# A pair's expert results added to their tokens by one-hot products, in place of rows scattered and read back

## The chip, the cores and the metric

One core of a Trainium2 chip. The metric is device time in microseconds (us) of one execution of the whole program; lower is better. Five engines work beside each other: TensorE (PE in the profile; its weight loads are PEld), VectorE (DVE), ScalarE (ACT), GpSimd (POOL) and SyncE (SP, which here issues the weight loads). They meet only through semaphores.

## What is computed

A backbone of two layers over 256 latent and 256 context tokens of width 1024. Layer 0 mixes tokens by windowed attention, layer 1 by a bidirectional linear recurrence; behind each stands a mixture of experts, and at the end a root-mean-square norm. What matters here is the mixture of layer 1, which sees the 256 latent tokens only. Its reference, cut to what matters:

```python
scores = sigmoid(t @ router_w)                       # 64 experts
idx    = top 8 of 64, within the best 4 of 8 groups
w      = scores[idx] / sum(scores[idx]) * 2.5
y      = (silu(t @ w_gate[e]) * (t @ w_up[e])) @ w_down[e] * w_b      # t: tokens of a block, one expert e
routed = zeros((T + 1, D)).at[tok_buf].add(y)        # each token: the sum of its 8 results
x      = x + g2 * (routed + shared)
return rms_norm(x, final_g)
```

256 tokens by 8 experts make 2048 results of 1024 numbers. All is float32; an expert has three matrices of 1 MB each.

## The kernel before

The program runs phases one behind the other, each a block in which every engine has its own list of instructions; a block ends when all engines have ended. `route_phase` chooses the experts and sorts (token, expert) entries into blocks of 64 slots; it also adds the shared expert into `g.x` and starts the first weight loads. `expert_pair_phase` (lines 1535 to 1796) is the stage of the change. `combine_phase` (1798 to 1880) sums the results, applies the gate, adds to the stream and does the final norm. `combine_phase` also serves layer 0, where nothing changes.

In `expert_pair_phase` a step handles a pair of blocks, 2 x 64 slots, one half of the 128 partitions each; there are 33 pairs. Slots without an entry have gain 0 and an index out of range. The first pair is peeled, the others run two to a turn of a loop. For pair i:

- GpSimd gathers 128 token rows into `xg` by an indirect DMA (`gather`, line 1617; rows out of range are skipped, and the tile was cleared once at line 1628). After the results are out of PSUM it scatters them to `y_rows` in device memory (`scatter`, line 1625), a row for each token and choice.
- TensorE (`step`, lines 1678 to 1704) projects gate and up (line 1674, weights loaded two pairs ahead into one of two buffers), transposes the tokens of pair i+1 (1666), looks up the slots of pair i+2 by a one-hot product (1654), transposes the hidden rows (1691), and multiplies by the down weights (1702), of which there is one buffer. Float32 matmuls show as two instructions each in the trace; projections and down product run as two halves of 64 columns side by side.
- ScalarE: SiLU (1725), half of the transposed tokens (1719), the transposed hidden rows (1728), half of the result (1732). VectorE: gain and product (1775), the other half of the tokens (1768), the indices (1760, 1763, 1781), the next one-hot (1748), the other half of the result (1783).
- SyncE issues the weight loads (926, 929, 932) in the order in which buffers come free: gate and up two pairs ahead, when the projections are done; down of pair i+1 when the down product of pair i is done.

All loads of the weights stand in one queue, in the order of issue. The order of work on each engine is written out by hand, as the lists show; nothing plans it at run time.

`combine_phase` reads `y_rows` back, four rows of a token at a time in four loads of 2 MB (line 1832); TensorE sums half of a tile's rows by products with the identity (1852), VectorE the other half (1867, 1869, 1872); then gate (1874), addition to the stream (1876) and the norm (ScalarE 328 and 330, VectorE 335 and 337), and the output is stored (1840).

Of the kernel before, what the change touches and what calls it, by code (L numbers as in the profile page):

```python
# [29 lines left out]
P = 128  # L30
# [1503 lines left out]

def expert_pair_phase(g, layer, tiles, routes, weights):

# [4 lines left out]
    S = slots_of(tiles)  # L1541
    last_token, last_row = tiles * P - 1, tiles * P * TOPK - 1
    half = (slice(0, S), slice(S, 2 * S))
    with ExitStack() as st:
        sb = lambda n, s, d=F32: st.enter_context(nc.sbuf_tensor(f"{tag}_{n}", s, d))
        sem = lambda n: g.sem(f"{tag}_{n}")
        wgu, wd = weights.wgu, weights.wd
        xg, ysb = g.h[:, 0, :], g.h[:, 2, :]
        xT = sb("xT", [P, KD, P])
        onehot = sb("onehot", [P, tiles, P], BF16)  # L1550
        meta = sb("meta", [P, NBMAX // 2, 3])
        gidx = sb("gidx", [P, 1], U32)
        sidx = sb("sidx", [P, 1], U32)
        act_g = sb("act_g", [P, FE])
        hid = sb("hid", [P, FE])
        hidT = sb("hidT", [P, KF, P])
        gathered, scattered, zeroed, issue = sem("gathered"), sem("scattered"), sem("zeroed"), sem("issue")
        onehot_s, meta_done, meta_v, idx_s = sem("onehot_s"), sem("meta_done"), sem("meta_v"), sem("idx_s")
        xT_turned, xT_a, xT_v = sem("xT_turned"), sem("xT_a"), sem("xT_v")
        gate_done, up_done, silued, hid_s = sem("gate_done"), sem("up_done"), sem("silued"), sem("hid_s")  # L1560
        hid_turned, hidT_s, y_done = sem("hid_turned"), sem("hidT_s"), sem("y_done")
        y_a, y_v, sidx_s = sem("y_a"), sem("y_v"), sem("sidx_s")
        GU, YB, XB, HB, MB = 0, 1, 3, 5, 6

# [10 lines left out]
        def peeled(i):  # L1575
            return isinstance(i, int) and i == 0

        with nc.Block() as block:
# [31 lines left out]
            @block.gpsimd  # L1610
            def _(pool):
                def gather(i):
                    pool.wait_ge(idx_s, i + 1)
                    if not peeled(i):
                        pool.wait_ge(xT_turned, i)
                    pool.sem_inc(issue, 1)
                    pool.indirect_dma_start(xg, None, g.h2_rows[0:tiles * P, :], bass.IndirectOffsetOnAxis(ap=gidx[:, 0:1], axis=0),
                                            bounds_check=last_token, oob_is_err=False).then_inc(gathered, 16)

                def scatter(i):  # L1620
                    pool.wait_ge(y_a, i + 1)
                    pool.wait_ge(y_v, i + 1)
                    pool.wait_ge(sidx_s, i + 1)
                    pool.sem_inc(issue, 1)
                    pool.indirect_dma_start(g.y_rows[0:tiles * P * TOPK, :], bass.IndirectOffsetOnAxis(ap=sidx[:, 0:1], axis=0), ysb, None,
                                            bounds_check=last_row, oob_is_err=False).then_inc(scattered, 16)

                pool.memset(xg, 0.0).then_inc(zeroed, 1)
                pool.wait_ge(zeroed, 1)
                turns = rounds(pool)  # L1630
                gather(0)
                gather(1)
                gather(2)
                scatter(0)
                with pool.Fori(0, turns) as m:
                    gather(2 * m + 3)
                    scatter(2 * m + 1)
                    gather(2 * m + 4)
                    scatter(2 * m + 2)
                pool.wait_ge(scattered, 32 * turns + 16)  # L1640
                pool.sem_inc(issue, 1)
                pool.wait_ge(gathered, 32 * turns + 48)
                pool.sem_inc(issue, 1)

            @block.tensor
            def _(pe):
# [21 lines left out]

                def project(q, r, a, loaded, done):
                    pe.wait_ge(loaded[q], 32 * r + 32)  # L1670
                    pe.sem_inc(issue, 1)
                    for k in range(KD):
                        for s in range(2):
                            last = pe.matmul(g.ps[half[s], GU, a * FE:(a + 1) * FE], xT[:, k, half[s]], wgu[:, q, s, a, k, :],  # L1674
                                             start=(k == 0), stop=(k == KD - 1))
                    last.then_inc(done, 1)

                def step(i, q, r):
# [5 lines left out]
                    project(q, r, 0, weights.gate_in, gate_done)  # L1684
                    project(q, r, 1, weights.up_in, up_done)
                    turn_tokens(i + 1)
                    slots(i + 2)
                    pe.wait_ge(hid_s, i + 1)
                    pe.sem_inc(issue, 1)
                    for j in range(KF):  # L1690
                        last = pe.transpose(g.ps[:, HB, j * P:(j + 1) * P], hid[:, j::KF], g.ident)
                    last.then_inc(hid_turned, 1)
                    pe.wait_ge(hidT_s, i + 1)
                    pe.wait_ge(weights.down_in, 32 * i + 32)
                    if not peeled(i):
                        pe.wait_ge(y_a, i)
                        pe.wait_ge(y_v, i)
                    pe.sem_inc(issue, 1)
# [12 lines left out]
                with pe.Fori(0, turns) as m:  # L1711
                    step(2 * m + 1, 1, m)
                    step(2 * m + 2, 0, m + 1)

            @block.scalar
            def _(act):
# [4 lines left out]
                def step(i):  # L1721
# [7 lines left out]
                    act.wait_ge(y_done, i + 1)  # L1729
                    if not peeled(i):  # L1730
                        act.wait_ge(scattered, 16 * i)
                    act.activation(ysb[:, 0:512], g.ps[:, YB, :], ACT.Copy).then_inc(y_a, 1)  # L1732

# [8 lines left out]
            def _(dve):  # L1742
# [23 lines left out]
                def tokens(i):  # L1766
                    dve.wait_ge(xT_turned, i + 1)
                    dve.tensor_copy(xT[:, 4:8, :], g.ps[:, XB + 1, :].rearrange("p (k c) -> p k c", c=P)).then_inc(xT_v, 1)  # L1768

                def step(i):  # L1770
                    dve.wait_ge(silued, i + 1)
                    dve.wait_ge(meta_v, 2 * i + 2)
                    if not peeled(i):
                        dve.wait_ge(hid_turned, i)
                    dve.scalar_tensor_tensor(hid[:], act_g[:], meta[:, bass.ds(i, 1), GAIN], g.ps[:, GU, FE:2 * FE], ALU.mult, ALU.mult).then_inc(hid_s, 1)  # L1775
                    tokens(i + 1)
                    indices(i + 2)
                    pick(i + 3)
                    if not peeled(i):
                        dve.wait_ge(scattered, 16 * i)  # L1780
                    dve.tensor_scalar(sidx[:], meta[:, bass.ds(i, 1), DEST], FAR, None, ALU.add).then_inc(sidx_s, 1)
                    dve.wait_ge(y_done, i + 1)
                    dve.tensor_copy(ysb[:, 512:D], g.ps[:, YB + 1, :]).then_inc(y_v, 1)  # L1783

# [3 lines left out]
                indices(1)  # L1788
                pick(2)
                tokens(0)  # L1790
                turns = rounds(dve)
                step(0)
                with dve.Fori(0, turns) as m:
                    step(2 * m + 1)
                    step(2 * m + 2)


def combine_phase(g, layer, tiles):
# [7 lines left out]
    with ExitStack() as st:  # L1806
# [15 lines left out]
        with nc.Block() as block:  # L1822
# [40 lines left out]
            def _(dve):  # L1863
                for t in range(tiles):
# [12 lines left out]
                    if t:  # L1877
                        dve.wait_ge(mod_in, 32 if layer == 0 else 16)
                        norm.dve(dve, t - 1)
                norm.dve(dve, tiles - 1)  # L1880


# [401 lines left out]
def backbone(nc, ins, table, out):  # L2284
    with ExitStack() as stack:
# [39 lines left out]
        with ExitStack() as layer:  # L2325
# [13 lines left out]
            with ExitStack() as moe:  # L2339
# [3 lines left out]
                turned.close()  # L2343
                expert_pair_phase(g, 1, LAT_TILES, routes, weights)
            combine_phase(g, 1, LAT_TILES)

# [69 lines left out]
```

## Time and profile before

| | us |
|---|---|
| median of 3 runs | 2253.72 (2251.86 to 2254.84) |
| the profiled execution | 2252.88 |
| its span in the trace | 2251.1 |
| second expert stage | about 1644 to 2205 |
| combination, norm and output | 2213 to 2251 |

| busy over the span | us | share |
|---|---|---|
| TensorE, matmul | 1853.2 | 82% |
| VectorE | 1116.1 | 50% |
| ScalarE | 797.5 | 35% |
| GpSimd | 315.8 | 14% |

The span runs from the first to the last instruction; the time of an execution has a little around it (1.8 us here). A busy share over the whole span mixes stages with different limits, so each stage is to be read by itself: busy time of each engine in the stretch, share of the 16 DMA engines, and which wait of the pacing engine ends last. The granted clock of TensorE is given as a share of full speed (0.5 is 1.2 GHz, 1.0 is 2.4 GHz).

### The profile page before, as it was taken

To read this page: it belongs to the slowest core of one execution; us is meant where nothing else is said; L and a number is where in the kernel's file an instruction comes from. 1 tells how busy PE (TensorE), PEld (TensorE's weight loads), DVE (VectorE), ACT (ScalarE), POOL (GpSimd) and SP (SyncE) were. 2 spreads that over 40 slices of the span, in tenths; PEclk is the share of its full clock that TensorE was granted. 3 is DMA by queue.
4 is the path that set the end of the run, shared out by engine and by line. 5 is a ranking of instruction groups with operands and counts; after the bars stand their busy time and mean duration, and the time that the engine had idled before them with its cause. 6 is when DMAs were issued, how large, how long until landed. Compare 5 with 4: busy or idle time off the path is not lost. (4 is left out here: it accounts for less than half of the span.)

```text
span 2251.1 us, 32259 instructions
## 1 busy us (share of the span) xinstructions
PE 1853.2 (82%) x9555; PEld 1210.6 (54%) x9556; DVE 1116.1 (50%) x1942; ACT 797.5 (35%) x1283; POOL 315.8 (14%) x333
## 2 busy tenths in 40 slices
PE   2899997979999999999966977638778778788884
PEld 0778853556767676766633961113445445455451
DVE  1425632477877777777836656891321111111113
ACT  1214511045656565666612547850101111111111
POOL 0220010011111111112211012220011111111110
PEclk9999988889999999999987988758879899999997
DMA  6860053258999999999956334304659999999984
GB/s 247 273 216 12 1 186 138 118 184 343 365 361 351 352 356 372 365 360 358 359 213 244 94 79 172 113 10 131 256 209 405 399 409 400 414 406 401 408 333 197
DMA packets 128296, 597.10 MB, mean 265 GB/s; under 512 B 32633, under 2 KB 51129, under 8 KB 67441
## 3 DMA queue, kind: packets, MB, share of 16 engines
q1 hardware_dynamic: 92512, 509.97, 58.7%
q0 software_dynamic: 35584, 84.32, 10.2%
q10 hardware_dynamic: 144, 2.10, 0.2%
q8 instruction: 32, 0.52, 0.1%
q14 instruction: 24, 0.19, 0.0%
HBM read 596.18 MB, written 56.20 MB: 290 GB/s over the span
## 5 line engine op out<-in xcount | busy, mean ns | idle before, releaser
L1484 DVE TENSOR_TENSOR m_w_lo<-mods,m_w_hi 128x1024 fp32r<-128x1024 f32 x264 | 311.6, 1222 | 27.4 <-ACT m_w_hi L1403 24.7
L1403 ACT ACTIVATE m_w_hi<-mods 128x1024 fp32r<-128x1024 f32 x264 | 263.7, 1049 | 13.9 <-PEq L995 12.0
L1355 PE MATMUL ps<-m_w_hi,m_x_hi 128*128 128x512 f32 x528 | 245.1, 464 | 5.6 <-DVE m_x_lo L1476 5.6
L1339 PE MATMUL ps<-m_wd,m_hidT 128*128 128x512 f32 x528 | 248.1, 592 | 0.9 <-DVE h L1492 0.9
L1702 PE MATMUL ps<-m_wd,m_hidT 128*64 128x512 f32 x528 | 163.5, 775 | 92.8 <-DMA m_wd<-in_moe_w_down 91.4
L1674 PE MATMUL ps<-m_wgu,m_xT 128*64 128x256 f32 x2112 | 236.7, 382 | 1.2 <-DVE m_xT L1768 1.2
L1674 PEld LDWEIGHTS ps<-m_wgu,m_xT 128*64 128x64 f32 x2112 | 175.0, 138 | 71.3 <-issue 21.2
L1355 PE MATMUL ps<-m_w_lo,m_x_hi 128*128 128x512 f32 x528 | 208.1, 394 | 0.0
L1355 PE MATMUL ps<-m_w_hi,m_x_lo 128*128 128x512 f32 x528 | 207.0, 392 | 0.0
L1702 PEld LDWEIGHTS ps<-m_wd,m_hidT 128*64 128x64 f32 x528 | 52.3, 176 | 180.2 <-issue 180.2
L1339 PEld LDWEIGHTS ps<-m_wd,m_hidT 128*128 128x128 f32 x528 | 95.5, 191 | 70.8 <-issue 63.6
L1775 DVE SCALAR_TENSOR_TENSOR m_hid<-m_act_g,m_meta,ps 128x256 f32<-128x256 f32 x33 | 15.8, 480 | 233.3 <-ACT m_act_g L1725 233.3
L1271 POOL DMA_INDIRECT h<-h_rows,m_gidx x69 | 72.8, 1055 | 342.8 <-DVE m_gidx L1468 337.8
L1355 PEld LDWEIGHTS ps<-m_w_hi,m_x_hi 128*128 128x128 f32 x528 | 100.0, 189 | 35.4 <-issue 21.3
L1355 PEld LDWEIGHTS ps<-m_w_hi,m_x_lo 128*128 128x128 f32 x528 | 100.3, 190 | 29.7 <-issue 15.3
L1355 PEld LDWEIGHTS ps<-m_w_lo,m_x_hi 128*128 128x128 f32 x528 | 99.5, 188 | 22.7
L328 ACT ACTIVATE squares<-x_stream 128x1024 bf16<-128x1024 f32 x16 | 16.9, 1053 | 264.4 <-DVE x_stream L867 140.8
L1783 DVE COPY h<-ps 128x512 f32<-128x512 f32 x33 | 22.8, 691 | 172.5 <-PE ps L1702 172.5
L1732 ACT ACTIVATE h<-ps 128x512 f32<-128x512 f32 x33 | 19.7, 597 | 246.2 <-PE ps L1702 246.2
L1280 POOL DMA_INDIRECT y_rows<-h,m_sidx x66 | 66.9, 1014 | 216.9 <-DVE h L1492 211.0
L1476 DVE TENSOR_TENSOR m_x_lo<-ps,m_x_hi 128x512 fp32r<-128x512 f32 x134 | 85.8, 681 | 5.9 <-ACT m_x_hi L1393 5.9
L1725 ACT ACTIVATE m_act_g<-ps 128x256 f32<-128x256 f32 x33 | 12.6, 383 | 210.9 <-PE ps L1674 210.9
(322 smaller groups left out, 3262.2 us busy)
## 6 DMA issues: line engine op xcount, KB each, us to landing
m_wd<-in_moe_w_down SPq DMA_DIRECT2D x132, 1024.0 KB, 11.1
mods<-in_moe_w_gate SPq DMA_DIRECT2D x66, 1024.0 KB, 7.0
mods<-in_moe_w_up SPq DMA_DIRECT2D x66, 1024.0 KB, 10.5
m_wgu<-in_moe_w_gate SPq DMA_DIRECT2D x66, 1024.0 KB, 11.2
m_wgu<-in_moe_w_up SPq DMA_DIRECT2D x66, 1024.0 KB, 13.5
c_rows<-y_rows SPq DMA_DIRECT2D x12, 2048.0 KB, 14.4
mods<-in_ada_w POOLq DMA_DIRECT2D x11, 1024.0 KB, 6.2
mods<-in_ada_w SPq DMA_DIRECT2D x11, 1024.0 KB, 4.9
```

Of the source, the lines that this page charges most:

```text
L328: act.activation(g.junk[:], g.x[:, t, :], ACT.Square, accum_out=g.sumsq[:, t:t + 1]).then_inc(self.squared, 1)
L1271: pool.indirect_dma_start(xg[q], None, g.h2_rows[0:tiles * P, :], bass.IndirectOffsetOnAxis(ap=gidx[q][:, 0:1], axis=0), bounds_check=last ...
L1280: pool.indirect_dma_start(g.y_rows[0:tiles * P * TOPK, :], bass.IndirectOffsetOnAxis(ap=sidx[q][:, 0:1], axis=0), ysb[q], None, bounds_che ...
L1339: last = pe.matmul(g.ps[0:S, YB + n, :], hidT[:, q, j, :], wd[:, q, j, n * 512:(n + 1) * 512], start=(j == 0), stop=(j == KF - 1))
L1355: last = pe.matmul(g.ps[0:S, GU, :].rearrange("p (a f) -> p a f", a=2), x[:, q, k, :], w[:, q, :, k, :], start=(k == 0 and n == 0), stop=( ...
L1403: act.activation(w_hi[:, q, :, k, :], wgu[:, q, :, k, :], ACT.Copy).then_inc(hi_s, 1)
L1476: dve.tensor_tensor(x_lo[:, q, ks, :], g.ps[:, XB + n, 0:4 * S].rearrange("p (k c) -> p k c", c=S), x_hi[:, q, ks, :].bitcast(F32), ALU.su ...
L1484: dve.tensor_tensor(w_lo[:, q, :, k, :], wgu[:, q, :, k, :], w_hi[:, q, :, k, :].bitcast(F32), ALU.subtract).then_inc(lo_s, 1)
L1674: last = pe.matmul(g.ps[half[s], GU, a * FE:(a + 1) * FE], xT[:, k, half[s]], wgu[:, q, s, a, k, :], start=(k == 0), stop=(k == KD - 1))
L1702: last = pe.matmul(g.ps[half[s], YB + n, :], hidT[:, j, half[s]], wd[:, s, j, n * 512:(n + 1) * 512], start=(j == 0), stop=(j == KF - 1))
L1732: act.activation(ysb[:, 0:512], g.ps[:, YB, :], ACT.Copy).then_inc(y_a, 1)
L1783: dve.tensor_copy(ysb[:, 512:D], g.ps[:, YB + 1, :]).then_inc(y_v, 1)
```

## The change

The results of a pair stay on the chip. ScalarE copies them from PSUM rounded to the short float format (float32r, `y_hi`), VectorE takes the remainder (`y_lo`). VectorE also makes a matrix `place` of 128 slots by 256 tokens, 1 where the slot's token is the column's. TensorE multiplies `place` with `y_hi` and `y_lo` into one PSUM bank (`put`), in four jobs (two tiles of tokens by two halves of the width), and VectorE adds each into a sum of 128x2x1024 in SBUF (`add`). The puts of pair i-1 stand among the work of pair i: the first behind the gate projection, the second in the middle of the up projection, the third behind the transposes of the tokens, the fourth behind those of the hidden rows. The sum and two tables are set up at the start of the stage. GpSimd issues no scatter, and clears the token tile ahead of each gather. `finish_phase` takes the place of `combine_phase` in layer 1. The diff, cut to its core:

```diff
--- before.py
+++ after.py
...
-def expert_pair_phase(g, layer, tiles, routes, weights):
+def expert_pair_phase(g, layer, tiles, routes, weights, total):
-        xg, ysb = g.h[:, 0, :], g.h[:, 2, :]
+        xg = g.h[:, 0, :]
-        sidx = sb("sidx", [P, 1], U32)
+        y_hi, y_lo = sb("y_hi", [P, D], F32R), sb("y_lo", [P, D], F32R)
+        place = sb("place", [P, tiles * P], F32R)
+        tokens_far = sb("tokens_far", [P, tiles, P])
+        jobs = [(t, n) for t in range(tiles) for n in range(2)]
+        J = len(jobs)
-        GU, YB, XB, HB, MB = 0, 1, 3, 5, 6
+        GU, YB, XB, HB, MB, TB = 0, 1, 3, 5, 6, 7
...
             def _(pool):
                 def gather(i):
-                    pool.wait_ge(idx_s, i + 1)
                     if not peeled(i):
                         pool.wait_ge(xT_turned, i)
                     pool.sem_inc(issue, 1)
+                    pool.memset(xg, 0.0).then_inc(zeroed, 1)
+                    pool.wait_ge(zeroed, i + 1)
+                    pool.wait_ge(idx_s, i + 1)
+                    pool.sem_inc(issue, 1)
                     pool.indirect_dma_start(xg, None, g.h2_rows[0:tiles * P, :], bass.IndirectOffsetOnAxis(ap=gidx[:, 0:1], axis=0),
                                             bounds_check=last_token, oob_is_err=False).then_inc(gathered, 16)
-                def scatter(i):
-                    pool.wait_ge(y_a, i + 1)
-                    pool.wait_ge(y_v, i + 1)
-                    pool.wait_ge(sidx_s, i + 1)
-                    pool.sem_inc(issue, 1)
-                    pool.indirect_dma_start(g.y_rows[0:tiles * P * TOPK, :], bass.IndirectOffsetOnAxis(ap=sidx[:, 0:1], axis=0), ysb, None,
-                                            bounds_check=last_row, oob_is_err=False).then_inc(scattered, 16)
-
-                pool.memset(xg, 0.0).then_inc(zeroed, 1)
-                pool.wait_ge(zeroed, 1)
                 turns = rounds(pool)
                 gather(0)
                 gather(1)
                 gather(2)
-                scatter(0)
                 with pool.Fori(0, turns) as m:
                     gather(2 * m + 3)
-                    scatter(2 * m + 1)
                     gather(2 * m + 4)
-                    scatter(2 * m + 2)
-                pool.wait_ge(scattered, 32 * turns + 16)
                 pool.wait_ge(gathered, 32 * turns + 48)
                 pool.sem_inc(issue, 1)
...
                         last = pe.transpose(g.ps[:, XB + k // 4, (k % 4) * P:(k % 4 + 1) * P], xg[:, k::KD], g.ident)
                     last.then_inc(xT_turned, 1)
-                def project(q, r, a, loaded, done):
+                def put(i, n, bank):
+                    t, half_of_d = jobs[n]
+                    if n == 0:
+                        pe.wait_ge(placed, i + 1)
+                        pe.wait_ge(y_low, i + 1)
+                    pe.wait_ge(added, J * i + n + 1)
+                    pe.sem_inc(issue, 1)
+                    for m, y in enumerate((y_hi, y_lo)):
+                        last = pe.matmul(g.ps[:, bank, :], place[:, t * P:(t + 1) * P], y[:, half_of_d * 512:(half_of_d + 1) * 512],
+                                         start=(m == 0), stop=(m == 1))
+                    last.then_inc(put_done, 1)
+                def project(q, r, a, loaded, done, inside=None):
                     pe.wait_ge(loaded[q], 32 * r + 32)
                     pe.sem_inc(issue, 1)
                     for k in range(KD):
+                        if k == KD // 2 and inside:
+                            inside()
                         for s in range(2):
                             last = pe.matmul(g.ps[half[s], GU, a * FE:(a + 1) * FE], xT[:, k, half[s]], wgu[:, q, s, a, k, :],
                                              start=(k == 0), stop=(k == KD - 1))
...
                     if not peeled(i):
                         pe.wait_ge(hid_s, i)
                     project(q, r, 0, weights.gate_in, gate_done)
-                    project(q, r, 1, weights.up_in, up_done)
+                    if peeled(i):
+                        project(q, r, 1, weights.up_in, up_done)
+                    else:
+                        put(i - 1, 0, TB)
+                        project(q, r, 1, weights.up_in, up_done, inside=lambda: put(i - 1, 1, TB))
                     turn_tokens(i + 1)
+                    if not peeled(i):
+                        put(i - 1, 2, TB)
                     slots(i + 2)
                     pe.wait_ge(hid_s, i + 1)
                     pe.sem_inc(issue, 1)
                     for j in range(KF):
                         last = pe.transpose(g.ps[:, HB, j * P:(j + 1) * P], hid[:, j::KF], g.ident)
                     last.then_inc(hid_turned, 1)
+                    if not peeled(i):
+                        put(i - 1, 3, TB)
                     pe.wait_ge(hidT_s, i + 1)
                     pe.wait_ge(weights.down_in, 32 * i + 32)
-                    if not peeled(i):
-                        pe.wait_ge(y_a, i)
-                        pe.wait_ge(y_v, i)
                     pe.sem_inc(issue, 1)
                     for j in range(KF):
                         for n in range(2):
...
                 with pe.Fori(0, turns) as m:
                     step(2 * m + 1, 1, m)
                     step(2 * m + 2, 0, m + 1)
+                for n in range(J):
+                    put(2 * turns, n, TB)
             @block.scalar
             def _(act):
...
                     act.wait_ge(hid_turned, i + 1)
                     act.activation(hidT[:], g.ps[:, HB, 0:KF * P].rearrange("p (j c) -> p j c", c=P), ACT.Copy).then_inc(hidT_s, 1)
                     act.wait_ge(y_done, i + 1)
-                    if not peeled(i):
-                        act.wait_ge(scattered, 16 * i)
-                    act.activation(ysb[:, 0:512], g.ps[:, YB, :], ACT.Copy).then_inc(y_a, 1)
+                    act.activation(y_hi[:], g.ps[:, YB:YB + 2, :].rearrange("p a b -> p (a b)"), ACT.Copy).then_inc(y_high, 1)
                 tokens(0)
                 turns = rounds(act)
...
                     dve.wait_ge(xT_turned, i + 1)
                     dve.tensor_copy(xT[:, 4:8, :], g.ps[:, XB + 1, :].rearrange("p (k c) -> p k c", c=P)).then_inc(xT_v, 1)
+                def add(i, n):
+                    t, half_of_d = jobs[n]
+                    part = total[:, t, half_of_d * 512:(half_of_d + 1) * 512]
+                    dve.wait_ge(put_done, J * i + n + 1)
+                    dve.tensor_tensor(part, part, g.ps[:, TB, :], ALU.add).then_inc(added, 1)
                 def step(i):
+                    if not peeled(i):
+                        add(i - 1, 0)
+                        add(i - 1, 1)
                     dve.wait_ge(silued, i + 1)
                     dve.wait_ge(meta_v, 2 * i + 2)
                     if not peeled(i):
                         dve.wait_ge(hid_turned, i)
                     dve.scalar_tensor_tensor(hid[:], act_g[:], meta[:, bass.ds(i, 1), GAIN], g.ps[:, GU, FE:2 * FE], ALU.mult, ALU.mult).then_inc(hid_s, 1)
                     tokens(i + 1)
+                    if not peeled(i):
+                        add(i - 1, 2)
                     indices(i + 2)
                     pick(i + 3)
                     if not peeled(i):
-                        dve.wait_ge(scattered, 16 * i)
-                    dve.tensor_scalar(sidx[:], meta[:, bass.ds(i, 1), DEST], FAR, None, ALU.add).then_inc(sidx_s, 1)
-                    dve.wait_ge(y_done, i + 1)
-                    dve.tensor_copy(ysb[:, 512:D], g.ps[:, YB + 1, :]).then_inc(y_v, 1)
+                        add(i - 1, 3)
+                    dve.tensor_scalar(place[:], tokens_far[:].rearrange("p t c -> p (t c)"), meta[:, bass.ds(i, 1), 0], None, ALU.is_equal).then_inc(placed, 1)
+                    dve.wait_ge(y_high, i + 1)
+                    dve.tensor_tensor(y_lo[:], g.ps[:, YB:YB + 2, :].rearrange("p a b -> p (a b)"), y_hi[:].bitcast(F32), ALU.subtract).then_inc(y_low, 1)
                 pick(0)
                 indices(0)
                 pick(1)
                 indices(1)
                 pick(2)
+                for t in range(tiles):
+                    dve.tensor_scalar(tokens_far[:, t, :], g.field("iota"), t * P - FAR, None, ALU.add).then_inc(far_s, 1)
+                dve.wait_ge(far_s, tiles)
+                dve.memset(total, 0.0).then_inc(added, 1)
                 tokens(0)
                 turns = rounds(dve)
                 step(0)
                 with dve.Fori(0, turns) as m:
                     step(2 * m + 1)
                     step(2 * m + 2)
+                for n in range(J):
+                    add(2 * turns, n)
...
+def finish_phase(g, tiles, total):
+        gain = st.enter_context(nc.sbuf_tensor("fin_gain", [P, D], F32))
+        norm = NormRows(g, "nf", None, lambda t: gain[:])
+        with nc.Block() as block:
+            @block.sync
+            def _(sp):
+                sp.dma_start(gain[:], g.ins["final_g"].partition_broadcast(P)).then_inc(gain_in, 16)
+                for t in range(tiles):
+                    sp.wait_ge(norm.ready, t + 1)
+                    sp.dma_start(g.out[0, t * P:(t + 1) * P, :], g.h[:, t, :]).then_inc(stored, 16)
+                sp.wait_ge(stored, 16 * tiles)
+            @block.scalar
+            def _(act):
+                for t in range(tiles):
+                    act.wait_ge(added, t + 1)
+                    norm.act(act, t)
+            @block.vector
+            def _(dve):
+                for t in range(tiles):
+                    dve.tensor_tensor(total[:, t, :], total[:, t, :], g.mod(t, GATE2), ALU.mult).then_inc(scaled, 1)
+                    dve.wait_ge(scaled, t + 1)
+                    dve.tensor_tensor(g.x[:, t, :], g.x[:, t, :], total[:, t, :], ALU.add).then_inc(added, 1)
+                dve.wait_ge(gain_in, 16)
+                for t in range(tiles):
+                    norm.dve(dve, t)
...
                 routes, weights = Routes(sb, 1, LAT_TILES), PairWeights(g, sb, 1)
                 route_phase(g, 1, LAT_TILES, routes, weights)
-                expert_pair_phase(g, 1, LAT_TILES, routes, weights)
-            combine_phase(g, 1, LAT_TILES)
+                total = g.h[:, 1::2, :]
+                expert_pair_phase(g, 1, LAT_TILES, routes, weights, total)
+            finish_phase(g, LAT_TILES, total)
```

## Rows read from the trace of the kernel before

**Rows 1.** Busy time by stretch: length, then busy us (count) of PE, PEld, DVE, ACT, POOL, clock, DMA share, GB/s

```profile
1665.00:1670.00 5.00, 4.56 (x27) 2.33 (x29) 1.87 (x8) 0.89 (x3) 0.99 (x1) 1.00 1.02 428
...
1800.00:2000.00 200.00, 161.31 (x1128) 100.20 (x1124) 34.57 (x111) 23.53 (x48) 24.30 (x25) 0.91 1.00 407
```

**Rows 2.** The waits of TensorE, 1660 to 2210 us: us in total, times, longest

```profile
PE ps L1702 <- DMA m_wd<-in_moe_w_down: 91.4, 31, 5.1
```

**Rows 3.** The DMA queues and issues, 1800 to 2150 us

```profile
q1 hardware_dynamic: 18089, 131.72, 92.1%
q0 software_dynamic: 6048, 10.75, 8.0%
...
h<-h_rows,m_gidx POOLq DMA_INDIRECT x22, 8.3
```

**Rows 4.** The timeline (start, us, instruction, [idle before]), TensorE's down products

```profile
1680.29 6.47 PE L1702 MATMUL ps<-m_wd,m_hidT 128*64 128x512 f32 x16 [2.31 <-DMA m_wd<-in_moe_w_down]
...
2184.34 5.33 PE L1702 MATMUL ps<-m_wd,m_hidT 128*64 128x512 f32 x16 [3.69 <-DMA m_wd<-in_moe_w_down]
...
2199.22 3.65 PE L1702 MATMUL ps<-m_wd,m_hidT 128*64 128x512 f32 x16 [0.78 <-ACT m_hidT L1728]
```

**Rows 5.** The timeline, the last pair, 2189 to 2199 us

```profile
2189.49 7.09 PE L1674 MATMUL ps<-m_wgu,m_xT 128*64 128x256 f32 x64
...
2196.51 0.97 PEld L1666 LDWEIGHTS ps<-table,h 128*128 128x128 f32 x8 [0.38 <-issue]
...
2197.74 0.68 DVE L1768 COPY m_xT<-ps 128x512 f32<-128x512 f32 x1
...
2197.96 0.47 PE L1691 MATMUL ps<-table,m_hid 128*128 128x128 f32 x2 [0.20 <-DVE m_hid L1775]
...
2198.48 0.38 ACT L1728 ACTIVATE m_hidT<-ps 128x256 f32<-128x256 f32 x1 [0.17 <-PE ps L1691]
```

**Rows 6.** The timeline, float32r matmuls of layer 0, around 800 us

```profile
800.14 0.39 PE L1355 MATMUL ps<-m_w_hi,m_x_hi 128*128 128x512 f32 x1
...
800.37 0.39 PE L1355 MATMUL ps<-m_w_hi,m_x_lo 128*128 128x512 f32 x1
```

**Rows 7.** Groups by line (count | busy, mean ns | idle before), whole span

```profile
L1403 ACT ACTIVATE m_w_hi<-mods 128x1024 fp32r<-128x1024 f32 x264 | 263.7, 1049 | 13.9 <-PEq L995 12.0
...
L1476 DVE TENSOR_TENSOR m_x_lo<-ps,m_x_hi 128x512 fp32r<-128x512 f32 x134 | 85.8, 681 | 5.9 <-ACT m_x_hi L1393 5.9
...
L759 DVE MEMSET lo_w<- 32x2048 f32 x4 | 7.1, 1765 | 1.9 <-issue 1.1 <-PEq L2122 0.8
```

**Rows 8.** The timeline, start of the stage, 1640 to 1661 us

```profile
1640.45 1.23 DVE L1093 TENSOR_TENSOR x_stream<-x_stream,h 128x1024 f32<-128x1024 f32 x1
...
1641.96 0.96 POOL L1628 MEMSET h<- 128x1024 f32 x1 [117.77 <-POOLq L995]
...
1652.94 0.69 DVE L1768 COPY m_xT<-ps 128x512 f32<-128x512 f32 x1
...
1653.73 9.56 PE L1674 MATMUL ps<-m_wgu,m_xT 128*64 128x256 f32 x64 [1.22 <-DVE m_xT L1768]
...
1660.10 0.89 SPq L926 DMA_DIRECT2D m_wgu<-in_moe_w_gate  x2
```

**Rows 9.** The timeline, end of the stage and combination

```profile
2202.99 0.60 ACT L1732 ACTIVATE h<-ps 128x512 f32<-128x512 f32 x1 [4.13 <-PE ps L1702]
...
2204.49 0.99 POOL L1625 DMA_INDIRECT y_rows<-h,m_sidx  x1 [3.73 <-DVE h L1783]
...
2213.17 0.81 SPq L1832 DMA_DIRECT2D c_rows<-y_rows  x2
...
2235.32 1.28 ACT L330 ACT_TABLE_LOAD   x1
...
2242.51 1.22 DVE L1874 TENSOR_TENSOR c_total<-c_total,mods 128x1024 f32<-128x1024 f32 x1
...
2245.03 1.06 ACT L328 ACTIVATE squares<-x_stream 128x1024 bf16<-128x1024 f32 x1 [8.12 <-DVE x_stream L1876]
```

More of the change, by code:

```diff
@@ L1541, in expert_pair_phase @@
     S = slots_of(tiles)
-    last_token, last_row = tiles * P - 1, tiles * P * TOPK - 1
+    last_token = tiles * P - 1
     half = (slice(0, S), slice(S, 2 * S))
@@ L1556, in expert_pair_phase @@
         hidT = sb("hidT", [P, KF, P])
-        gathered, scattered, zeroed, issue = sem("gathered"), sem("scattered"), sem("zeroed"), sem("issue")
+        gathered, zeroed, issue = sem("gathered"), sem("zeroed"), sem("issue")
         onehot_s, meta_done, meta_v, idx_s = sem("onehot_s"), sem("meta_done"), sem("meta_v"), sem("idx_s")
@@ L1561, in expert_pair_phase @@
         hid_turned, hidT_s, y_done = sem("hid_turned"), sem("hidT_s"), sem("y_done")
-        y_a, y_v, sidx_s = sem("y_a"), sem("y_v"), sem("sidx_s")
-        GU, YB, XB, HB, MB = 0, 1, 3, 5, 6
+        y_high, y_low, placed = sem("y_high"), sem("y_low"), sem("placed")
+        put_done, added, far_s = sem("put_done"), sem("added"), sem("far_s")
+        GU, YB, XB, HB, MB, TB = 0, 1, 3, 5, 6, 7
         def rounds_after_first(eng):
@@ L1633, in _ @@
                 gather(2)
-                scatter(0)
                 with pool.Fori(0, turns) as m:
                     gather(2 * m + 3)
-                    scatter(2 * m + 1)
                     gather(2 * m + 4)
-                    scatter(2 * m + 2)
-                pool.wait_ge(scattered, 32 * turns + 16)
-                pool.sem_inc(issue, 1)
                 pool.wait_ge(gathered, 32 * turns + 48)
@@ L1880, in _ @@
                 norm.dve(dve, tiles - 1)
+def finish_phase(g, tiles, total):
+    nc = g.nc
+    with ExitStack() as st:
+        gain = st.enter_context(nc.sbuf_tensor("fin_gain", [P, D], F32))
+        gain_in, stored = g.sem("fin_gain_in"), g.sem("fin_stored")
+        scaled, added = g.sem("fin_scaled"), g.sem("fin_added")
+        norm = NormRows(g, "nf", None, lambda t: gain[:])
[21 more added lines that the diff above has]
+                    norm.dve(dve, t)
 BA, BX, LAM, CW, CB = 0, 2, 4, 6, 10
```

## The prediction

> **What bounds the kernel now.** I read the table of busy time by stretch first. In the second expert stage (about 1644 to 2205 us) the row of 1800 to 2000 us has the DMA engines at a share of 1.00 and 407 GB/s, TensorE busy 161 of 200 us, VectorE 35, ScalarE 24, GpSimd 24 [rows 1]. So the stage is paced by transfers. The waits say which: TensorE waited 31 times, 91.4 us in all, for the down weights before line 1702 [rows 2]. The list of DMA queues splits the 350 us from 1800 to 2150: the hardware queue (weights) took 92.1% of the 16 engines' time, the software queue (22 gathers, 21 scatters) 8.0%, together 100% [rows 3]. The starts of the down product give the period: from 1680.29 to 2184.34 us are 30 pairs, 504.05 / 30 = 16.80 us each [rows 4].
>
> TensorE's own chain is shorter. The last pair did not wait for weights: 2184.34 to 2199.22 is 14.88 us, of which the down product at 2184.34 took 5.33 where the one at 2199.22 took 3.65 (part of it ran at the lower of the two clocks, after an idle stretch); at full clock the chain is 14.88 - 1.68 = 13.2 us [rows 4]. Nearly 3.6 us per pair are to spare. After the last pair comes the combination: TensorE ends at 2199.22 + 3.65 = 2202.87, the span at 2251.1, so 48.2 us of tail [rows 4, 9].
>
> **Part 1, the scatters go.** 8.0% of 350 us is 28.0 us for 43 software transfers, 0.65 us each of all 16 engines' time [rows 3]. Nothing else limits the period as long as TensorE's chain is below it, and the next down load is issued about 11 us before it lands, so the queue never runs dry. 31 scatters (pairs 0 to 30) are sent before the last down load that TensorE waits for. Gain 31 x 0.65 = 20.2 us, period 16.80 - 0.65 = 16.15. Bounds: nothing, if weights move no faster without scatters; at most, weights at the 428 GB/s of 1665 to 1670 us, when mostly weights moved [rows 1]: 131.72 MB / 21 = 6.27 MB per pair, 14.65 us instead of 15.35, another 0.7 us per pair or 22 us. I take 20.2, since the 5 us stretch is short and the gathers stay.
>
> **Part 2, what is added to each pair.** TensorE gets eight single-pass matmuls of 128x512 (four puts of two). Line 1355 runs the same kind and type: starts 0.23 us apart at full clock [rows 6], so a put holds TensorE 0.45 us. Put 0 stands behind the gate projection. It needs ScalarE's rounded copy of 128x1024 (1.05 us by line 1403) and VectorE's remainder (2 x 0.68 by line 1476, taken as 1.25) [rows 7], done 2.5 us after the down product; the gate projection lasts half of 7.09 = 3.5 us [rows 5], so it hides them, with 1 us over. Put 1 comes 1.8 us later in the up projection, and its accumulator bank is free again after 0.69 us of adding; no wait. With 0.1 us each for the wait instruction these two add 1.1 us. Put 2 follows the transposes; nobody waits but TensorE. Put 3 waits for the add of put 2, which VectorE does only behind its copy of the transposed tokens: in the last pair's times that copy ends at 2197.74 + 0.68 = 2198.42, the add at 2199.15, put 3 at 2199.75, where the down product began at 2199.22 [rows 4, 5]; so puts 2 and 3 together cost 0.6 us, the rest falls into the wait for ScalarE's transposed hidden rows (2198.48 + 0.38). Chain: 13.2 + 1.1 + 0.6 = 14.9 us, under 16.15. In the 31 pairs bound by transfers this costs nothing; without that cover it is 1.7 us per pair. It shows once, in the last pair: +1.7. It also shortens idle stretches, so fewer down products should drop to the lower clock; that too is hidden.
> VectorE gets four adds of 0.69, one product-mask of 256 columns and the remainder instead of a copy: 2.8 + 0.4 + 0.6, some 3.7 us on 3.5 busy per 16.8; no bound. The add in front of the index arithmetic makes the gather about 0.7 us later; a gather lands 8.3 us after issue [rows 3] of a period of 16.15, and goes out some 4 us after the transposes, so about 4 us are left. GpSimd's memset of the token tile, 0.96 us [rows 8], runs after the transposes while VectorE still computes the indices (about 1.2 us): hidden, or at worst 1 us later for the same gather. Down products no longer wait for evacuation; put 0's wait has covered that.
>
> **Part 3, the start.** VectorE now fills two token tables and clears a 128x2048 sum before its first copy of transposed tokens (1652.94), on which the first projection (1653.73) hangs, and on that the third pair's gate load at 1660.10, with which the saturated stretch begins [rows 8]. Clearing: 1.8 us by line 759's 2048 columns [rows 7]; tables about 0.25 each. +2.3 us, bounds 1.2 (clearing at twice the rate) and 5 (if the later start leaves TensorE longer at the lower clock, at which most of its first projection of 9.56 us already ran).
>
> **Part 4, the tail.** After the last down product: copy and remainder 0.1 + 1.05 + 0.1 + 1.25 = 2.5 us, then four rounds through one bank: two matmuls 0.6, add 0.69, two hand-overs 0.15, 1.45 us each; 1.9 at the lower clock. Four are 5.8 to 7.6, taken as 6.5: 9.0 us. The change of phase is 0.4: at the phase before, GpSimd's memset began 0.3 us after VectorE's last add [rows 8]; bounds 0 and 4. Before, the same point (line 1832's first issue at 2213.17) was 10.3 us after the down product, scatter included [rows 9]. The new phase: multiply, add, multiply, add at 1.22 each [rows 9] are 5.0 us. ScalarE squares tile 0 from 2.5 (1.06, 0.2 for the sum, 1.28 for the table load, 0.3), so it ends tile 1 at 7.1 instead of the 1.5 us behind the second add that it takes now. Before, from the second multiply (2242.51) to the end were 8.6 us [rows 9]; now 2.5 + 8.6 + 0.6 = 11.7. The 512 KB of gains are moved by then. Tail 9.0 + 0.4 + 11.7 = 21.1 against 48.2: gain 27.1, bounds 22 and 29.
>
> **Sum.** The profiled execution took 2252.88 us (span 2251.1): 2252.88 - 20.2 + 1.7 + 2.3 - 27.1 = 2209.6. The median of the runs is 0.84 above that execution, so 2210.
>
> **A rule that speaks against it.** Going from the half-width projections to the full-width transposes, TensorE shows no gap: the projections run from 2189.49 for 7.09 us, the weight load of the transposes begins at 2196.51, after 0.38 us without a weight load [rows 5]. The Trainium skill's page "TensorEngine Tiling (Array Packing)", Key Properties, says that changing the tiling mode drains the engine. Puts 0 and 1 lie inside half-width work, four more changes per pair; by that rule something like the 0.38 us would be lost at each, by the row nothing. That makes it a rival, below.
>
> **The rivals.**
> - TensorE's chain becomes the bound. Four changes of array width at 0.38 us are 1.5 us: chain 16.4, over 16.15; 0.25 x 30 + 1.5 + 2210 = 2219. With slow down products added (1.7 us in many pairs now [rows 4]) up to 17.0: 2236. Against: no gap between the kinds now, and less idle time to lose the clock in.
> - The weights gain more than the scatters' own time, as 428 GB/s hints: half of that bound, 0.35 x 31 = 11 us, gives 2199. Against: a share of 1.00 at 407 GB/s in all long stretches.
> - The change doesn't shorten the stage, since the weight queue alone sets the period and scatters fit in between: 2210 + 20 = 2230. Against: both queues' shares add up to 100%.
> - Slower than before: the one accumulator bank makes TensorE and VectorE take turns. If VectorE, in order behind its waits for the activation and the transposes, is late at each add, every put costs a full round of 1.45 us and puts 1 to 3 hold up projections and down product: 13.2 + 4 x 1.45 = 19.0 us, 2.85 more than 16.15, 31 times: 2210 + 88 = 2298. It decides from a chain of 16.15 + 43 / 31 = 17.6 us on. Against: 1.8 us of projection stand between puts 0 and 1, 2 us between 1 and 2.
>
> **Chances.** Forecast 0.64 (own range 2203 to 2217), TensorE's chain 0.18, faster weights 0.10, unshortened stage 0.04, slower 0.04. Under 0.2% (4.5 us) this kernel can't be told from unchanged; only tails of the rivals end there, 0.01. Faster 0.95, slower 0.04. Range 2195 to 2229.
>
> **What would show it.** Right: starts of the down product 16.1 us apart, DMA share still 1.00, TensorE still waiting about 1 us for down weights in most pairs, software queue's share about half, first gate load of the third pair near 1662.5, 21 us from the last down product to the end. Wrong: no more waits for down weights (TensorE is the bound); a period still of 16.8 with those waits (scatters cost nothing); a first projection much later than 1656; rounds of the last four adds over 2 us.

## The result and the profile after

The changed kernel takes 2198.26 us (median of 4 runs, 2193.9 to 2200.84) against 2254.28 (4 runs); the ratio is 0.975, 95% interval 0.973 to 0.977. Timed again later it took 2195.66 (5 runs), ratio 0.976 (0.975 to 0.978). Forecast were 2210 us and a range of 2195 to 2229: right in sign and range, but the gain is 56 us, not 44. The profiled execution took 2200.84 us, span 2199.0; it is the slowest of the four, so the profiles differ by less (52.1 us) than the medians.

The waits of TensorE in the stage (us in total, times, longest), against [rows 2]:

```profile
PE ps L1670 <- DVE h L1786: 20.4, 32, 0.7
PE ps L1714 <- DMA m_wd<-in_moe_w_down: 5.6, 10, 0.7
```

91.4 us of waiting for down weights have become 5.6. Line 1670 is the put, and what it waits for is the add of the put before it. The row of 1800 to 2000 us and the DMA queues of 1800 to 2120 us, against [rows 1, 3]:

```profile
1800.00:2000.00 200.00, 188.38 (x1303) 109.72 (x1299) 79.22 (x164) 30.27 (x52) 24.32 (x25) 1.00 1.01 413
```

```profile
q1 hardware_dynamic: 17503, 127.45, 96.7%
q0 software_dynamic: 3003, 5.28, 4.4%
```

The engines of the DMA are as full as before, the weights have 96.7% of them instead of 92.1%, and TensorE is granted full speed, here and in every stretch from 1670 to 2175 us. Some starts of the down product, against [rows 4]:

```profile
1685.46 3.65 PE L1714 MATMUL ps<-m_wd,m_hidT 128*64 128x512 f32 x16
...
1716.44 3.65 PE L1714 MATMUL ps<-m_wd,m_hidT 128*64 128x512 f32 x16
...
1731.52 0.40 PE L1670 MATMUL ps<-m_y_lo,m_place 128*128 128x512 f32 x1
1732.03 3.65 PE L1714 MATMUL ps<-m_wd,m_hidT 128*64 128x512 f32 x16
1748.22 3.65 PE L1714 MATMUL ps<-m_wd,m_hidT 128*64 128x512 f32 x16 [0.62 <-DMA m_wd<-in_moe_w_down]
...
2172.60 0.40 PE L1670 MATMUL ps<-m_y_lo,m_place 128*128 128x512 f32 x1
2172.93 3.65 PE L1714 MATMUL ps<-m_wd,m_hidT 128*64 128x512 f32 x16
```

From 1732.03 the next start is 16.2 us away, with a wait for weights that the list holds. From 1716.44 it is 15.6 us away, and that period has a wait too, too short for the list: the down product starts 0.51 us behind the last matmul of the put, where it starts 0.33 us behind it in the last period (2172.60 to 2172.93). That last period, 15.4 us, is TensorE's own chain (15.4 and 15.5 by turns in the loop). The mean is (2157.52 - 1685.46) / 30 = 15.74 us: TensorE is 0.3 us per pair faster than the transfers, and waits a little for them in most pairs.

Since the code up to the stage is the same in all kernels here, but its end moved between 1637.8 and 1643.7 us from profile to profile, I count from that end (VectorE's last addition of the shared expert). In us, from one profile of each kernel:

| kernel | first projection | second down product | 30 periods (mean) | last period | last down product to end | all |
|---|---|---|---|---|---|---|
| before | 12.1 | 38.6 | 504.1 (16.80) | 14.9 | 51.9 | 609.4 |
| changed | 15.2 | 42.5 | 472.1 (15.74) | 15.4 | 26.1 | 556.1 |
| changed, again | 15.4 | 42.7 | 472.3 (15.74) | 15.4 | 25.3 | 555.7 |
| before, no scatter | 12.2 | 37.7 | 473.2 (15.77) | 14.9 | 47.8 | 573.6 |
| before, empty scatter | 12.0 | 37.6 | 477.7 (15.92) | 13.2 | 52.0 | 580.5 |
| changed + scatter | 15.1 | 42.6 | 507.2 (16.91) | 15.4 | 25.9 | 591.0 |
| changed + second gather | 17.1 | 43.6 | 500.8 (16.69) | 15.4 | 25.7 | 585.4 |
| three banks | 15.2 | 42.0 | 471.5 (15.72) | 15.0 | 21.5 | 549.9 |
| clearing on GpSimd | 12.2 | 39.3 | 471.5 (15.72) | 15.4 | 26.1 | 552.2 |
| clearing on GpSimd, again | 11.9 | 39.2 | 471.4 (15.71) | 15.4 | 26.1 | 552.0 |
| both | 11.8 | 38.6 | 471.3 (15.71) | 14.9 | 21.5 | 546.4 |
| both, again | 12.1 | 38.7 | 471.7 (15.72) | 14.9 | 21.9 | 547.2 |

The 52.1 us between the two spans are: +1.2 ahead of the stage (not the change's), +3.9 to the second down product, -32.0 over 30 periods, +0.5, -25.8 at the end.

One period of the changed kernel on TensorE and VectorE, against [rows 5]:

```profile
2149.06 0.50 PE L1670 MATMUL ps<-m_y_hi,m_place 128*128 128x512 f32 x1
2149.39 0.40 PE L1670 MATMUL ps<-m_y_lo,m_place 128*128 128x512 f32 x1
2149.72 1.95 PE L1681 MATMUL ps<-m_wgu,m_xT 128*64 128x256 f32 x16
...
2154.14 1.16 PE L1659 MATMUL ps<-table,h 128*128 128x128 f32 x8
...
2155.47 0.68 DVE L1780 COPY m_xT<-ps 128x512 f32<-128x512 f32 x1
...
2156.07 0.68 DVE L1786 TENSOR_TENSOR h<-h,ps 128x512 f32<-128x512 f32 x1
...
2156.89 0.47 PE L1670 MATMUL ps<-m_y_hi,m_place 128*128 128x512 f32 x1 [0.68 <-DVE h L1786]
...
2157.52 3.65 PE L1714 MATMUL ps<-m_wd,m_hidT 128*64 128x512 f32 x16
```

Put 0 holds TensorE from 2149.06 to 2149.72; its matmuls start 0.33 us apart, where line 1355's did 0.23 [rows 6]. Put 3 waits, as worked out, for the add behind the token copy. The start of the stage, against [rows 8]:

```profile
1654.08 0.94 DVE L1814 TENSOR_SCALAR m_tokens_far<-table 128x128 f32<-128x128 f32 x2
1655.52 1.76 DVE L1816 MEMSET h<- 128x2048 f32 x1 [0.49 <-DVE m_tokens_far L1814]
1657.31 0.69 DVE L1780 COPY m_xT<-ps 128x512 f32<-128x512 f32 x1
1658.11 9.69 PE L1681 MATMUL ps<-m_wgu,m_xT 128*64 128x256 f32 x64 [4.34 <-DVE m_xT L1780]
```

And its end, against [rows 9]: the second and third of the four rounds, then the new phase.

```profile
2181.33 0.76 PE L1670 MATMUL ps<-m_y_hi,m_place 128*128 128x512 f32 x1 [0.87 <-DVE h L1786]
2181.89 0.63 PE L1670 MATMUL ps<-m_y_lo,m_place 128*128 128x512 f32 x1
2182.55 0.69 DVE L1786 TENSOR_TENSOR h<-h,ps 128x512 f32<-128x512 f32 x1 [1.38 <-PE ps L1670]
2183.39 0.77 PE L1670 MATMUL ps<-m_y_hi,m_place 128*128 128x512 f32 x1 [0.87 <-DVE h L1786]
...
2187.70 1.23 DVE L1942 TENSOR_TENSOR h<-h,mods 128x1024 f32<-128x1024 f32 x1 [0.32 <-PEq L1583]
```

### The profile page after: what moved, and what is told of

The parts are those of the page before. It is cut to its first block and busy times, and to the rows that moved or that the text cites. A ratio compares the mean times of both kernels' runs of the same rounds, so it can differ in the third digit from the quotient of the medians.

```text
span 2199.0 us, 33098 instructions
## 1 busy us (share of the span) xinstructions
PE 1885.2 (86%) x9787; PEld 1211.7 (55%) x9788; DVE 1221.3 (56%) x2071; ACT 811.3 (37%) x1283; POOL 321.7 (15%) x334
## 5 line engine op out<-in xcount | busy, mean ns | idle before, releaser
L1403 ACT ACTIVATE m_w_hi<-mods 128x1024 fp32r<-128x1024 f32 x264 | 263.9, 1049 | 20.8 <-PEq L995 11.9
L1681 PE MATMUL ps<-m_wgu,m_xT 128*64 128x256 f32 x2112 | 251.1, 385 | 4.3 <-DVE m_xT L1780 4.3
L1681 PEld LDWEIGHTS ps<-m_wgu,m_xT 128*64 128x64 f32 x2112 | 160.9, 138 | 96.2 <-issue 46.7
L1786 DVE TENSOR_TENSOR h<-h,ps 128x512 f32<-128x512 f32 x132 | 90.5, 685 | 124.8 <-PE ps L1670 123.8
L1271 POOL DMA_INDIRECT h<-h_rows,m_gidx x69 | 79.4, 1151 | 349.9 <-DVE m_gidx L1468 345.4
L1714 PE MATMUL ps<-m_wd,m_hidT 128*64 128x512 f32 x528 | 120.6, 597 | 7.1 <-DMA m_wd<-in_moe_w_down 5.6
L1621 POOL MEMSET h<- 128x1024 f32 x35 | 33.3, 952 | 525.4 <-PE ps L1659 407.0
L1744 ACT ACTIVATE m_y_hi<-ps 128x1024 fp32r<-128x1024 f32 x33 | 33.8, 1023 | 157.6 <-PE ps L1714 157.6
L1670 PE MATMUL ps<-m_y_hi,m_place 128*128 128x512 f32 x132 | 65.3, 495 | 25.7 <-DVE h L1786 23.0
```

Source lines behind the costliest of these rows:

```text
L1271: pool.indirect_dma_start(xg[q], None, g.h2_rows[0:tiles * P, :], bass.IndirectOffsetOnAxis(ap=gidx[q][:, 0:1], axis=0), bounds_check=last ...
L1403: act.activation(w_hi[:, q, :, k, :], wgu[:, q, :, k, :], ACT.Copy).then_inc(hi_s, 1)
L1670: last = pe.matmul(g.ps[:, bank, :], place[:, t * P:(t + 1) * P], y[:, half_of_d * 512:(half_of_d + 1) * 512], start=(m == 0), stop=(m == 1))
L1714: last = pe.matmul(g.ps[half[s], YB + n, :], hidT[:, j, half[s]], wd[:, s, j, n * 512:(n + 1) * 512], start=(j == 0), stop=(j == KF - 1))
L1744: act.activation(y_hi[:], g.ps[:, YB:YB + 2, :].rearrange("p a b -> p (a b)"), ACT.Copy).then_inc(y_high, 1)
L1786: dve.tensor_tensor(part, part, g.ps[:, TB, :], ALU.add).then_inc(added, 1)
```

## The experiments

The question was why a scatter is worth 1.06 us per pair when its own packets take 0.65. Theory A: beside its own time it costs the weights theirs. Theory B: the rest comes from TensorE's steadier rhythm at full clock, which sends the down loads off more evenly. All four kernels were timed on one chip, before at 2252.33.

**1. Before, without scatters.**

```diff
-                    pool.indirect_dma_start(g.y_rows[...], ..., ysb, None, ...).then_inc(scattered, 16)
+                    pool.sem_inc(scattered, 16)
```

> The kernel before without the scatters (GpSimd only counts the semaphore up; the combination then sums rows that this layer did not write). TensorE's work, its idle stretches and its falls to the lower clock stay. Theory A, a scatter costs the weight transfers more than its own packets' time: the period of the down products falls from 16.80 us to about 15.75, as in the changed kernel, 31 x 1.05 = 33 us less in the stage, and some 5 us less at the change of phase: about 2216 us. Theory B, the scatter costs only its 0.65 us and the other 0.4 us came from TensorE's steadier rhythm at full clock: period 16.15, about 2228 us.

2215.89 us, ratio 0.984 (0.982 to 0.986); period 15.77. Its queues from 1800 to 2120 us and TensorE's waits from 1680 to 2170:

```profile
q1 hardware_dynamic: 17548, 127.79, 96.7%
q0 software_dynamic: 2880, 5.09, 4.2%
```

```profile
PE ps L1700 <- DMA m_wd<-in_moe_w_down: 68.9, 30, 3.8
```

TensorE idles 2.3 us per pair and still falls to the lower clock (0.94 granted from 1800 to 2120 us, 0.91 before), and yet the period is the changed kernel's. Theory B falls: the stage's gain is the scatter's alone.

**2. Before, with empty scatters.**

```diff
-  dve.tensor_scalar(sidx[:], meta[:, bass.ds(i, 1), DEST], FAR, None, ALU.add)
+  dve.tensor_scalar(sidx[:], meta[:, bass.ds(i, 1), DEST], 2 * FAR, None, ALU.add)
```

> The kernel before with every row of the scatters out of range: descriptors are made and sent, no result is written (the combination sums rows that this layer did not write). If the written data are what costs (A): period near that without scatters, 15.8 to 16.0 us, about 2220 us. If the descriptors of a software transfer cost as much as its data: about 16.3 us, 2235 us. Theory B says no lower than 16.15.

2221.87 us, ratio 0.986 (0.985 to 0.988); period 15.92. Twice the packets of experiment 1 and the same megabytes:

```profile
q1 hardware_dynamic: 17404, 126.74, 95.9%
q0 software_dynamic: 5760, 5.10, 4.8%
```

Descriptors without data cost 0.15 us per pair over none at all, the data 16.80 - 15.92 = 0.88. Every instruction and every wait of the kernel before is still there, so it is not the order of the work or the waits on the scatter that cost. Its last period, with both down products at full clock, is 13.2 us: the chain that the prediction worked out for TensorE.

**3. The changed kernel, with the scatter beside it.**

```diff
+  def scatter(i):
+      pool.wait_ge(y_high, i + 1)
+      pool.wait_ge(sidx_s, i + 1)
+      pool.indirect_dma_start(g.y_rows[...], ..., y_hi[:].bitcast(F32), None, ...).then_inc(scattered, 16)
```

> The changed kernel, with each pair's rounded results also scattered to device memory as before (nobody reads them). Theory A: the period goes from 15.74 us to 16.8, 31 x 1.06 = 33 us more, about 2231 us. Theory B: TensorE stays steady, so the scatter costs its own packets' time alone, 15.74 + 0.65 = 16.4 us, about 2219 us.

2229.14 us, ratio 0.989 (0.987 to 0.991); period 16.91.

```profile
q1 hardware_dynamic: 16312, 118.79, 91.3%
q0 software_dynamic: 5472, 9.81, 8.0%
```

A scatter added costs 1.17 us per pair, one removed 1.03. The weights move at 118.79 MB / (0.913 x 320 us) = 407 GB/s of their own time here, at 412 in the changed kernel and 413 in experiment 1; and the shares add up to 99.3% here and to 101.1% in the changed kernel.

**4. The changed kernel, every gather twice.**

```diff
+  pool.indirect_dma_start(xg2, None, g.h2_rows[...], gidx, ...).then_inc(again, 16)
```

> The changed kernel with every gather made twice, the second into a tile that nobody reads: as many software packets and bytes as with a scatter, but read from device memory. If the extra cost is that of writes to device memory: the period grows by the packets' own 0.65 to 0.7 us, to about 16.4, 2219 us. If it is that of any software transfer beside the weights: as with the scatter, 16.8 us, 2231 us.

2227.41 us, ratio 0.989 (0.987 to 0.990); period 16.69.

```profile
q1 hardware_dynamic: 16502, 120.15, 91.1%
q0 software_dynamic: 5472, 9.97, 8.2%
```

A read costs 0.95 us per pair where its packets take about 0.68, a surcharge of 0.3 us, against 0.5 for the write that was added to the same kernel. The queues say in what the two differ. The DMA engines are less full in both (99.3% for 101.1%). But beside the second read the weights move at 120.15 MB / (0.911 x 320 us) = 412 GB/s, as in the changed kernel, and beside the writes at 407. So 0.3 us come with any second software transfer of data here, and 0.2 with writes alone. Neither forecast was right: 2227 us lies 8 over the one and 4 under the other.

**5. Three banks.** The second and third put go to the two result banks, the first and fourth to their own.

```diff
+        BANKS = (7, 1, 2, 7)
-                    pe.wait_ge(added, J * i + n + 1)
+                    if n == 0: pe.wait_ge(added, J * i + 1)
+                    if n == 3: pe.wait_ge(added, J * i + 2)
...
+                    if not peeled(i): pe.wait_ge(added, J * (i - 1) + 4)      # ahead of the down product
```

> The changed kernel with the puts spread over three PSUM banks (their own bank for the first and the fourth, the two result banks, free by then, for the second and third), so that no put waits for the add just ahead of it. TensorE's chain falls from 15.5 to about 14.9 us. Theory A, the transfers still set the mean period (15.74): TensorE waits again for down weights, 0.6 to 0.8 us per pair, the stage stays within 2 us; only the last pair (0.6) and the four rounds at the end (about 3 us) gain: about 2195 us. Rival, TensorE's chain is the bound now: period 14.9 to 15.0, 30 x 0.7 = 21 us less and the same gains at the end: about 2174 us.

2192.1 us, ratio 0.9737 (0.9724 to 0.975), beside before at 2251.54.

```profile
PE ps L1721 <- DMA m_wd<-in_moe_w_down: 31.6, 29, 1.5
PE ps L1721 <- DVE h L1793: 0.9, 3, 0.3
```

The last period shows the shorter chain, 14.95 us; the mean stays at 15.72, and what TensorE saves comes back as waits for down weights, 15.72 - 14.95 = 0.77 us per pair (the list's 31.6 us also hold 0.3 us per pair that TensorE waits for VectorE's add in any case, as in the last period). So the transfers bound the changed kernel. A second sign of it: seven of the 30 periods are of 16.2 us in the changed kernel, and the same seven are here and in experiment 1 (which have one or two more at the start), whatever TensorE has to do; why these, the runs don't show. The end gains 4.6 us against the changed kernel's first profile and 3.8 against its second, in which the clock fell later.

**6. The sum cleared by GpSimd, the tables made later.**

```diff
                 gather(1)
+                pool.memset(total, 0.0).then_inc(added, 1)
                 gather(2)
```

> The changed kernel with the sum cleared by GpSimd behind its second gather, and VectorE's token tables made behind its first copy of tokens. If the 3.2 us between VectorE's third one-hot and that copy delay the whole saturated stage one for one: 3.2 us less, about 2195 us. If the later start is absorbed by the weights that were prefetched: no change, 2198 us.

2195.5 us, ratio 0.9752 (0.9739 to 0.9766). The first projection comes 3 us earlier and the stage with its end is 3.9 us shorter by its profile (552.2 against 556.1), but the runs don't resolve it. So it was timed again beside the changed kernel:

> The changed kernel itself, timed beside the two below: 2198 us as before, so that the variants are compared on one chip.

> The sum cleared by GpSimd, again: 3.2 us under the changed kernel of the same call if the start delays the stage one for one; the same time as it if the start is absorbed.

2195.66 us (2194.56 to 2202.34) for the changed kernel, 2196.16 for this one, ratios 0.9761 (0.9747 to 0.9775) and 0.9752 (0.9739 to 0.9765). Inconclusive end to end: what comes ahead of the stage varies by more than the gain (it ended at 1637.8 us in the one profile and at 1643.3 in the other). By the profiles (552.2 and 552.0 against 556.1 and 555.7) nothing of the start is absorbed.

**7. Both.**

> Both changes of the two kernels before this one. If they are independent their gains add up: about 2191 us; if the transfers take back what the banks bring in the stage, the same, since only its two ends gain.

2189.06 us, ratio 0.9724 (0.9711 to 0.9737). And again:

> Three banks and the clearing on GpSimd, again: about 7 us under the changed kernel of the same call if both gains hold and add up, about 4 us if only the banks gain.

2189.26 us, 0.9722 (0.9709 to 0.9735), 6.4 us under the changed kernel timed beside it; by the profiles 546.4 and 547.2 us from the mark to the end. This is the fastest version. By the profiles the end and the start each give their part; by the runs the start's part isn't shown.

## Why the prediction was right, and where it was not

- **How near it was.** The forecast of 2210 us missed by 12 us, and its own range of 2203 to 2217 didn't hold the result. The whole range did, by 3 us at its lower end. Sign and bottleneck were right for the reasons given; the size was not.
- **What bounds the stage: right.** Transfers did, and do (experiment 5). TensorE's added work is hidden: with its puts (changed) and without (experiment 1) the period is the same, 15.74 and 15.77.
- **Part 1, the size of the scatters: the term that failed.** I took 8.0% of 350 us over 43 transfers, 0.65 us each, 20.2 us in all; they were worth 1.06 us per pair, 32.0 us over the 30 periods. The step at fault is that both queues' shares add up to 100%, and that a scatter therefore costs its own share and no more. A share counts the time of a queue's own packets and not what they do to those of the other queue, nor how full the engines are. From before to changed the 1.06 us are 0.65 of the scatters' packets, 0.2 in which the weights' own packets take less time (they move at 412 GB/s; before it was 120.23 MB in 92.0% of 320 us, 408), and 0.2 by which the engines are fuller (101.1% for 100.0%). The rival of faster weights (2199 us, given 0.10) priced the missing 0.4 us well, at 0.35; its mechanism is at most half of them, so part of that was luck.
- **Part 2, the chain: 14.9 us forecast, 15.4 found** (last period). A put among half-width projections holds TensorE 0.66 us instead of 0.45; both stretch the projections from 7.02 to 8.66 us, start to start (1719.90 to 1728.56), 1.6 us where I added 1.1. Part of it is the wider spacing of the matmuls in a put. Behind put 0 the next half-width matmul comes 0.33 us after the second one, behind put 2 a full-width one 0.23 us (2139.84 to 2140.07), so a return to half width costs about 0.1 us, not the 0.38 us of that rival. The Trainium skill's page "TensorEngine Tiling (Array Packing)", Key Properties, says that a change of mode drains the engine; the trace agrees in kind, with 0.1 us. The 0.6 us of puts 2 and 3 was right. In the last pair I added 1.7 us to a period of 14.88 that held 1.68 us of slow down product, which is now fast: my own chain gave +0.0 there; it was +0.5.
- **The clock: right in kind.** Every down product took 3.65 us, where many took 5 to 6.5; it paid nothing inside the stage.
- **Part 3, the start: +2.3 forecast, +3.1 to 3.3 found.** The clearing was 1.76 us as taken; the tables took 0.94 with a wait of 0.49 behind them, where I took 0.5 for all. Experiment 6 shows it, by its profiles, passing through to the stage's end.
- **Part 4, the tail: 27.1 forecast, 25.8 found.** The rounds took 2.06 us each, at the lower clock (0.50 granted from 2179 to 2188 us), not 1.45 to 1.9. That is one of my signs of being wrong, though it cost only 1.6 us. In the second profile the first two rounds ran at full clock, 1.57 us each. The phase after them began 0.3 us after the last add and took 11.3 us, for 11.7.
- **The rivals.** TensorE's chain did not become the bound, though it came within 0.3 us of the mean. Taking turns on one bank made TensorE wait 0.6 us per pair (20.4 us in all), of which 0.46 lengthened its chain (15.41 against 14.95 in experiment 5), far from the full rounds of the slower case.
- Against the forecast of -43.3 us for the profiled execution the terms are off by +0.9 (start), +0.7 (the first period, 15.5 instead of 14.9 us), -11.8 (30 periods), -1.2 (last period), +1.3 (tail) and +1.2 (ahead of the stage): -52.2, as measured but for rounding. One term holds nearly all of it.

## What to carry to other kernels

Where a stage is bound by full DMA engines, price a small transfer that is removed from them by more than its own share of packet time: here 1.4 to 1.8 times. Where the freed time then meets another engine that is nearly as slow, shortening that engine gives nothing inside the stage, but does at both ends, where nobody covers it. Compare variants of a late stage from a mark at its start, when what lies ahead varies by more than they differ.

## What the runs showed of the hardware

- A software transfer of 62 rows of 4 KB per pair, beside a saturated queue of weights, costs 0.95 us (read) or 1.03 to 1.17 us (written), for 0.65 to 0.69 us of its own packets; with no row in range 0.15 us. Beside rows that are written the weights move at 407 (experiment 3) and 408 GB/s (before) of their own time, and at 412 or 413 in every kernel here that writes none, the one with two reads per pair included. With the scatter added to the changed kernel the 1.17 us are 0.66 of its packets, 0.2 by which the weights' 6.29 MB move slower (407 GB/s for 412), and 0.3 by which the DMA engines are less full (99.3% for 101.1% of 16.9 us). Why they do either, the runs don't show.
- Two single-pass float32r matmuls of 128x512 start 0.31 to 0.34 us apart in a put and 0.23 in a long run of them at the same clock. It is the first spacing behind other work or a wait that is wider: in the tail with three banks, where the puts follow each other, the first is 0.31 us and the next three 0.23. Why, the runs don't show.
- After 2.7 us without work TensorE ran the tail's first put at the lower clock in the changed kernel's first profile (0.76 us for its first matmul). In its second profile, after 2.8 us, the first two puts ran at the higher clock (0.47 us) and the third at the lower (0.77), and with three banks the third was the first to slow down (0.63 us): much the same idle stretch, another moment of the fall.
